# Down-projection weights of a grouped mixture-of-experts loaded as four consecutive rows per partition

## The reference

```
def expert_block(args):
    xt, e = args
    hid = jax.nn.silu(xt @ w_gate[e]) * (xt @ w_up[e])     # (tokens, 512)
    return hid @ w_down[e]                                  # (tokens, 1024)
...
x = layer_norm(DEEPNORM_ALPHA * x + ffn, ln_g[i, 1], ln_b[i, 1])
```

## Time and profile before

| | us |
|---|---|
| median of 3 runs | 1344.19 (1343.43 to 1345.04) |
| the profiled execution, its own time | 1343.79 |
| its span, first to last instruction | 1341.9 |
| PE busy | 1035.6 (77%) |
| DVE busy | 305.8 (23%) |
| ACT busy | 176.3 (13%) |
| DMA moved | 450.93 MB in 74813 packets, mean 336 GB/s |

### The profile page before, as it was taken

The page is one execution under the profiler, slowest core; times in us unless marked ns, Lnnn a source line. Parts: engine busy times, 40 slices in busy tenths (PEclk is TensorE's granted clock), DMA queues, the critical chain, the costliest instruction groups (busy, mean ns, idle before and its releaser), DMA issues. The chain is left out here.

```text
span 1341.9 us, 16976 instructions
## 1 busy us (share of the span) xinstructions
PE 1035.6 (77%) x7062; PEld 561.7 (42%) x7062; DVE 305.8 (23%) x874; ACT 176.3 (13%) x438; POOL 40.6 (3%) x106
## 2 busy tenths in 40 slices
PE   7999889996676567666599899999966675675654
PEld 5675444353233234232388655544442342242321
DVE  0025521111111111111321675411111111111114
ACT  1013210010000000000111552201000000000000
POOL 2001010000000000000000110100000000000000
PEclk9999999998778888788699999999988788788787
DMA  9933638999999999999955206198999999999993
GB/s 334 384 126 126 220 138 366 397 421 420 425 420 422 422 421 419 419 420 418 372 209 202 113 1 241 69 423 344 419 420 420 419 421 424 423 421 422 420 418 125
DMA packets 74813, 450.93 MB, mean 336 GB/s; under 512 B 3739, under 2 KB 9980, under 8 KB 58348
## 3 DMA queue, kind: packets, MB, share of 16 engines
q1 hardware_dynamic: 72716, 442.96, 81.1%
q0 software_dynamic: 2016, 6.81, 1.6%
HBM read 448.68 MB, written 1.07 MB: 335 GB/s over the span
## 5 line engine op out<-in xcount | busy, mean ns | idle before, releaser
L689 PE MATMUL bank<-ring,work 128*32 128x256 f32 (+1 forms) x3520 | 353.7, 517 | 205.2 <-DMA ring<-in_moe_w_up 102.0
L689 PEld LDWEIGHTS bank<-ring,work 128*32 128x32 f32 (+1 forms) x3520 | 178.3, 143 | 385.2 <-issue 364.4
L1175 DVE TENSOR_TENSOR work<-work,bank 128x256 f32<-128x256 f32 (+1 forms) x32 | 15.6, 488 | 660.5 <-PE bank L689 660.5
L529 PE MATMUL bank<-xT,ring 128*128 128x256 f32 x512 | 116.7, 389 | 2.8 <-DMA ring<-in_moba_w_in 2.1
L724 PE MATMUL bank<-ring,work 128*32 128x512 f32 x768 | 104.5, 693 | 10.1 <-DMA ring<-in_moe_w_down 10.1
L529 PEld LDWEIGHTS bank<-xT,ring 128*128 128x128 f32 x512 | 99.1, 195 | 18.9 <-issue 3.9
L1183 DVE TENSOR_TENSOR acc<-acc,bank 128x512 f32<-128x512 f32 x128 | 82.0, 683 | 39.7 <-PE bank L741 32.2
L662 PE MATMUL bank<-xT,work 128*128 128x256 f32 x320 | 75.7, 392 | 1.2 <-DVE acc L1183 0.7
L662 PEld LDWEIGHTS bank<-xT,work 128*128 128x128 f32 x320 | 61.2, 196 | 18.6 <-issue 8.2
L1441 ACT COPY work<-bank 128x256 f32<-128x256 f32 (+1 forms) x32 | 13.6, 426 | 362.4 <-PE bank L697 362.4
L609 PE MATMUL bank<-ring,work 128*128 128x512 f32 x128 | 57.3, 599 | 1.1 <-issue 1.1
(11 more groups left out here) (204 smaller groups left out, 726.8 us busy)
## 6 DMA issues: line engine op xcount, KB each, us to landing
ring<-in_moe_w_up SPq DMA_DIRECT2D x64, 2048.0 KB, 19.5
ring<-in_moe_w_down SPq DMA_DIRECT2D x64, 2048.0 KB, 20.3
ring<-in_moe_w_gate SPq DMA_DIRECT2D x60, 2048.0 KB, 19.2
ring<-in_moba_w_in SPq DMA_DIRECT2D x6, 2048.0 KB, 26.8
ring<-in_nsa_w_in SPq DMA_DIRECT2D x5, 2048.0 KB, 20.4
ring<-in_moba_w_out SPq DMA_DIRECT2D x2, 2048.0 KB, 19.0
bias<-in_moe_w_gate SPq DMA_DIRECT2D x2, 2048.0 KB, 8.0
softmax_area<-in_moe_w_gate SPq DMA_DIRECT2D x2, 2048.0 KB, 8.0
```

The lines of the kernel that those rows point to most:

```text
L529: last = mm(bank[g % 2][:, n * SEQ:(n + 1) * SEQ], pick_cols(w, t), xT[:, t, :], start=(t == 0), stop=(t == KT - 1))
L689: last = mm(bank[2 + k][row:row + cap, 0:width], xgT[:, t, at + e * cap:at + (e + 1) * cap], w[e][:, t, part * width:(part + 1) * width], ...
```

## The change

A down weight is now read with four consecutive rows, 16 KB in one piece, on each partition. Partition p then holds rows 4p to 4p+3, so block m of the slot meets the hidden columns 4p+m: the transposes take every fourth column of `hid`. For the narrow pairs, where the halves are stacked, this takes eight 64x64 matmuls against the identity (four m, two halves) in place of two 128x128 transposes; the result fills the same 256 columns of PSUM and of `hidT`, in another order. The down matmuls keep their number and shapes. The overflow path follows the same order.

```
                 if kind == "down":
-                    return src.rearrange("a (m p) n -> p (a m) n", p=P)
+                    return src.rearrange("a (p m) n -> p (a m) n", m=FT)
...
+        hidT_narrow = work[:, 7296:7552].rearrange("p (m s) -> p m s", s=2 * CAP_NARROW)
...
             def transpose_hidden(l, i):
                 pe.wait_ge(hid_ready[l], i + 1)
                 after(pe, acc_added[l], 4 * (i - 1) + 1)
-                for m in range(FT if i < WIDE else 2):
-                    last = tr(bank[4][:, m * P:(m + 1) * P], hid[:, m * P:(m + 1) * P], ident)
+                if i < WIDE:
+                    for m in range(FT):
+                        last = tr(bank[4][:, m * P:(m + 1) * P], hid[:, m::FT], ident)
+                else:
+                    for m in range(FT):
+                        for half in range(2):
+                            at = slice(64 * half, 64 * half + 64)
+                            last = mm(bank[4][at, m * 64:(m + 1) * 64], hid[at, m:FF // 2:FT], ident[at, at], start=True, stop=True)
                 last.then_inc(hidT_psum[l], 1)
...
                 for m in range(FT):
-                    col = 64 * (m // 2)
                     for n in range(2):
                         for e in range(2):
                             row = 64 * n + CAP_NARROW * e
                             last = mm(bank[5][row:row + CAP_NARROW, :],
-                                      hidT[:, m % 2, col + CAP_NARROW * e:col + CAP_NARROW * (e + 1)],
+                                      hidT_narrow[:, m, CAP_NARROW * e:CAP_NARROW * (e + 1)],
                                       w[e][:, m, n * 512:(n + 1) * 512], start=(m == 0), stop=(m == FT - 1))
...
-                                        last = mm(bank[2 + k][:, mt * P:(mt + 1) * P], w[:, t, mt * P:(mt + 1) * P], ov_xgT[:, t, :],
+                                        last = mm(bank[2 + k][:, mt * P:(mt + 1) * P], w[:, t, mt::FT], ov_xgT[:, t, :],
```

## The result

The changed kernel takes 1333.61 us, median of 5 runs (1333.19 to 1334.75), beside 1344.19 for the kernel before (5 runs, 1340.92 to 1349.94). The ratio is 0.992, 95% interval 0.9898 to 0.9941: 0.8% faster. The forecast was 1333.8. The profiled execution took 1333.61 us with a span of 1331.8.

A forecast was written before the change was run, and what follows sets the result against it. Loads were taken to bound two stretches of 395 us, PE the rest. 1343.8 - 10.9 for larger pieces + 0.5 for a fetch = 1333.4, with 0.4 to the median 1333.8 us; range 1330.5 to 1336.5.

The forecast's parts named there:

- The bound: Loads set the time in two stretches of 395 us, pairs 3 to 15 of each layer; elsewhere loads hide.
- 26 x 0.42 = 10.9 us: Gain in the two full stretches: 26 pairs, each down interval falling from 10.21 to 9.79 us.
- Rivals 1 and 2: Down loads' slower rate: not from pieces, no gain, 1344.7 us, chance 0.06; or only half from pieces, 1339.2 us, chance 0.08.
- rival 3: Full stretches: busy share is right and pair 2 counts, 28 x 0.57 = 16.0 us gained, 1328.7 us; chance 0.06.
- The doubt about pair 2: Pair 2's down loads may join the full stretch; then 28 pairs count, 0.8 us more gain.
- The 3 cycles of the Trainium skill: Overhead per packet in down loads: 48 x 3.5 ns = 0.17 us a pair, 4.4 us in all, 1340.3 us.
- Narrow transposes: Narrow pairs: eight 64x64 matmuls take 0.6 us more, at most 1.56, hidden behind PE's waits; price 0.
- Wide transposes: Wide pairs: four transposes reading every fourth column cost no more; price 0, upper end 3.1 us.
- Instruction fetch, 0.5 us: PE's stream: 288 more instructions, one more fetch delaying a load, charged 0.5 us, between 0 and 1.2.
- rival 4: Full stretches: instruction fetches meeting 16 KB pieces delay landings, 12 at 1.2 us, 14.4 us, 1348.2 us; chance 0.04.
- The joints: Ends of full stretches: all later work moves with the last down landing, so the gain passes; no loss counted.
- the forecast's own sign: Layer's end: the forecast is wrong if PE no longer waits before the last down matmuls.

The follow-up runs named there:

- experiment 1: Kernel before with only the down loads changed to 16 KB pieces, compute in its old order (wrong output): 1331.64 us, ratio 0.9906.
- experiment 2: Changed kernel with the down loads turned back to four 4 KB pieces, new compute kept (wrong output): 1346.26 us, ratio 1.0016.
- 3: Changed kernel with each partition's four consecutive down rows laid down in reverse, so loads have 4 KB pieces again: 1345.08 us, ratio 1.001.
- 7: Changed kernel with the ring's gate and up loads cut into 4 KB pieces, down loads whole: 1356.32 us, ratio 1.0077.
- 5: Changed kernel with each down load in 256 pieces of 8 KB: 1337.46 us, ratio 0.9933.
- 6: Changed kernel with each down load in 1024 pieces of 2 KB: 1361.89 us, ratio 1.0112.
- 10: Changed kernel with all narrow transposes issued twice in every narrow pair: 1331.77 us, ratio 0.9906.
- experiment 4: Changed kernel run again unaltered, as yardstick in two groups: 1335.03 us (ratio 0.9923) and 1333.55 us (ratio 0.9918).
- 8: Changed kernel with four narrow-transpose matmuls issued twice in 11 pairs of layer 0: 1330.39 us (ratio 0.988), again 1330.80 us (ratio 0.9899).

## Why the prediction held

**The bound.** Right. The loads set the time in two stretches of 395 us and nowhere else: the changed loads alone shorten exactly those two (experiment 1), and the changed compute alone leaves them (2).

**26 x 0.42 = 10.9 us.** Right: 10.7 to 11.4 us in the two stretches over the three traces of the changed kernel, 11.1 in experiment 1 (394.80 + 394.60 less 389.12 + 389.19). The 0.42 is a cost of pieces: not of where the rows lie (3), not of the tensor or its slots (7), and in proportion to their number (5, 6). Rivals 1 and 2 fall with that. So does rival 3, by the size of the gain: its 16.0 us did not come, the busy share overstated it. The doubt about pair 2 would have made 11.7 us; the stretches speak for 26 pairs, but their spread leaves room for part of it.

**The 3 cycles of the Trainium skill.** The Trainium skill (DMA: Bandwidth & Descriptors, "Why small descriptors are slow (HBM only)") has a fixed overhead of about 3 cycles for each packet, 3.5 ns by the estimate in the forecast. Sign and form are right; the runs show 8 to 10 ns for each piece of 2 to 16 KB, so the measurement decides.

**Narrow transposes.** 0.76 us more, where 0.6 was taken and 1.56 was the upper end; price 0 is right. Twice their number costs nothing that can be measured (10).

**Wide transposes.** Nearly right: 0.75 and 0.63 us for the first two pairs' four, against 0.66 and 0.60 before; the first stretch grew by 0.3 us, most of it elsewhere.

**Instruction fetch, 0.5 us.** Mis-sized, and by a wrong count: 672 instructions, not 288, three fetches more, not one. It was priced as a delay of a load. Such delays exist in both kernels: of the 536 intervals between landings that the PE timelines of all traces show, 42 are more than 0.6 us longer than their kind (0.7 to 1.6 us), and each of the 42 has an instruction fetch inside it. Another 237 have a fetch as well and are not late, so most fetches cost nothing. This is the fetch queue (packets, MB, share) in the 11.19 us from 1091.94 to 1103.13 of the changed kernel:

```profile
q8 instruction: 1, 0.02, 0.6%
```

But the change added nothing there. What a stretch takes beyond its 39 intervals was 7.5 and 7.3 us before (394.8 and 394.6 less 13 x 29.79) and is 7.7 and 7.4 us after (389.47 and 389.23 less 13 x 29.37). So rival 4 had a mechanism that these traces bear out, and the wrong price: single delays are a little longer with the large pieces (up to 1.5 us in the changed kernel, up to 1.2 before), their sum is not. What the longer stream brought instead is the stall of 1.7 to 1.9 us on PE itself after layer 0, in all eight traces with the changed kernel's stream length (the changed kernel three times, experiments 2, 3, 5, 6 and 7), and in none of the others.

**The joints.** This step failed in part, by the forecast's own sign. A stretch was to end with the landing of the down weights; in the profiled execution it ends with the chain of PE and VectorE behind the up landing. At a layer's last pair 0.75 us of wait should have been left (1.17 less 0.42), and experiment 1 has 0.79 there. What ate it is PE's clock: the last up matmuls took 6.29 us behind their landing, at a granted clock of 0.57, where they had taken 5.35 at 0.68. The down matmuls behind them then ran without a wait at 3.64 us, not 5.0 to 5.2, which gives 1.4 to 1.6 us at each of two places. That gain was not forecast. It is not the change's alone either: experiment 2, with the old loads, has 3.64 us at both ends, experiment 1, with the old transposes, at one, and the changed kernel in experiment 4 lacks it after layer 0 (5.32 us behind a wait of 0.49). Why a trace falls one way or the other is not shown. The unforecast gain and the stall, forecast too small, nearly cancel. The total is therefore closer to the forecast (0.2 us) than its parts deserve; in the other two groups the changed kernel had 1335.03 and 1333.55 us.

**What stays open.** What the stall waits for, and why it comes with one stream length and not with three longer ones; and the 2.1 us in the first stretch of experiments 6 and 8. The stretch between the full ones varies from 284.4 to 288.6 us among three executions of the changed kernel; part is PE's clock after the joint (the 64 projection matmuls took 15.5 to 17.1 us), the rest I did not trace.

## What to carry to other kernels

Where a stretch has a DMA share of 1, compare landings of loads of equal size and different shape in the trace of the kernel as it is: the interval of the better shape is the forecast for the worse, and the difference times the number of such intervals in that stretch is the gain. Count only the stretches where the DMA queue never runs dry, and find the work that hides the price on the other engines. At the margin left by such a gain, the length of the instruction stream counts: 336 instructions more by the end of a layer came with a stall at the joint, where nothing hides it, while 416, 512 and 720 more came with none. Look for it in the trace.

## What the runs showed of the hardware

- A 2 MB load costs 8 to 10 ns for each piece on its DMA engine beside the time for its bytes, between 2 and 16 KB: two loads took 9.79, 9.95, 10.21 and 10.80 us at 16, 8, 4 and 2 KB.
- A plain float32 matmul of 64x64 stands in the trace as two matmuls and two weight loads, a transpose as one; sixteen such took 1.17 us, 73 ns each.
- A weight load that reads every fourth column took 205 ns, mean of 32 (L699), against 140 ns for the contiguous one (L697 of the kernel before), with almost no effect on the group's time (0.63 against 0.60 us for four).
- TensorE stood still for 1.7 to 1.9 us in the middle of a group of transposes, waiting for nothing that the profile shows, in eight of eight traces with one stream length and in none of six with others.
- Late weight loads go with instruction fetches: all 42 intervals between landings that are 0.7 to 1.6 us too long have one inside, and none of the 257 intervals without a fetch is over 0.6 us too long. Another 237 intervals with a fetch are not late either.
